# Expert inputs gathered as quarter rows per block of 32 tokens, turned by VectorE and scaled by GpSimd

## The reference, cut to what matters

```python
x = layer_norm(alpha * x + g2 * hier_moe(modulate(x, sh2, sc2), *moe_w), ln2_g[i], ln2_b[i])
# modulate(u, shift, scale) = normalize(u) * (1 + scale) + shift
# routed_experts: for each token t and each of its two experts e, weighted by gate:
#   h = silu(t @ w_gate[e]) * (t @ w_up[e]);   y = h @ w_down[e]
```

## Time and profile before

| | us |
|---|---|
| median of three runs | 1712.03 (1709.75 to 1712.45) |
| span of the profiled execution | 1710.9 |
| expert stage, first transposes to last down product | 1186 to 1648 |
| TensorE busy in the span | 1513.6 |
| VectorE, ScalarE, GpSimd busy | 928.0, 691.7, 209.5 |

### The profile page before, as it was taken

One profiled execution on the slowest core, in us unless ns is written; L12 is line 12 of the kernel. 1 busy time (PEld: TensorE's weight loads), 2 busy tenths in 40 slices (PEclk: granted clock), 3 DMA queues, 4 the chain that ended last, 5 costly groups with the idle time before them and its releaser, 6 DMA issues. The chain is left out here.

```text
span 1710.9 us, 47254 instructions
## 1 busy us (share of the span) xinstructions
PE 1513.6 (88%) x19436; PEld 1110.0 (65%) x19436; DVE 928.0 (54%) x1855; ACT 691.7 (40%) x1585; POOL 209.5 (12%) x274
## 2 busy tenths in 40 slices
PE   4799998999968899977999979873999999999868
PEld 2588886779857788864666667762555555555433
DVE  5798752331125556649999846666151543545416
ACT  5544431012334455435777724432142423443321
POOL 0000101000034535404000000000000000000014
PEclk9899999999977999999999989885999999999989
DMA  9312315551133344231011033316849589999976
GB/s 363 115 62 90 114 62 205 175 165 39 59 114 109 115 127 127 84 104 50 26 54 34 13 121 148 136 76 265 354 136 409 222 324 413 400 401 418 409 251 251
DMA packets 115267, 305.34 MB, mean 178 GB/s; under 512 B 11010, under 2 KB 57682, under 8 KB 106074
## 3 DMA queue, kind: packets, MB, share of 16 engines
q1 hardware_dynamic: 93178, 244.95, 37.8%
q0 software_dynamic: 10336, 46.67, 7.8%
q10 hardware_dynamic: 11520, 10.49, 2.0%
HBM read 256.41 MB, written 45.67 MB: 177 GB/s over the span
## 5 line engine op out<-in xcount | busy, mean ns | idle before, releaser
L2747 PE MATMUL psum<-now_hidden,i_xm 128*32 128x256 f32 x4992 | 291.0, 385 | 9.8 <-DVE now_hidden L2849 6.4
L2747 PEld LDWEIGHTS psum<-now_hidden,i_xm 128*32 128x32 f32 x4992 | 160.0, 111 | 132.0 <-issue 27.6
L2759 PE MATMUL psum<-now_down,i_hT 128*32 128x256 f32 x2464 | 147.7, 379 | 5.8 <-ACT now_down L2810 5.8
L2865 DVE TENSOR_TENSOR i_h<-i_silu,psum 128x128 f32<-128x128 f32 x78 | 22.2, 285 | 219.6 <-ACT i_silu L2803 219.6
L2793 ACT ACTIVATE i_xm<-psum,run_mod 128x128 f32<-128x128 f32 x163 | 63.3, 457 | 152.1 <-issue 125.7
L2759 PEld LDWEIGHTS psum<-now_down,i_hT 128*32 128x32 f32 x2464 | 81.4, 110 | 58.9 <-ACT now_down L2810 9.2
L2849 DVE COPY now_hidden<-raw_hidden 128x1024 f32 x168 | 104.4, 693 | 21.2 <-DMA raw_hidden<-in_w_up 11.9
L124 PE MATMUL psum<-hT_head,wm_head 128*128 128x512 f32 (+1 forms) x256 | 96.6, 377 | 11.8 <-DVE hT_rest L415 7.5
L1918 PE MATMUL psum<-dkT,f_qT 64*128 64x512 f32 (+1 forms) x384 | 90.7, 580 | 18.4 <-ACT f_E L1968 15.9
L1968 ACT ACTIVATE f_E<-psum,f_mx 128x1280 f32<-128x1280 f32 (+2 forms) x96 | 92.8, 971 | 19.9 <-DVE f_mx L2029 19.1
L124 PE MATMUL psum<-hT_head,wm_rest 128*128 128x512 f32 (+1 forms) x256 | 94.6, 369 | 0.0
(11 more groups left out here) (378 smaller groups left out, 3049.7 us busy)
## 6 DMA issues: line engine op xcount, KB each, us to landing
raw_hidden<-in_w_gate SPq DMA_DIRECT2D x22, 2048.0 KB, 25.0
raw_hidden<-in_w_up SPq DMA_DIRECT2D x22, 2048.0 KB, 29.5
raw_down<-in_w_down SPq DMA_DIRECT2D x22, 2048.0 KB, 19.9
wa_late<-in_w_ada POOLq DMA_DIRECT2D x16, 1024.0 KB, 6.9
yb<-i_y ACTq DMA_DIRECT2D x80, 128.0 KB, 11.5
wa<-in_w_ada SPq DMA_DIRECT2D x8, 1024.0 KB, 13.7
wt<-in_w_in SPq DMA_DIRECT2D x4, 2048.0 KB, 8.8
wm<-in_w_in SPq DMA_DIRECT2D x12, 512.0 KB, 3.8
```

Source lines behind the costliest of these rows:

```text
L2747: last = nc.tensor.matmul(by_blocks(hidden_bank(s)[j * SUB:(j + 1) * SUB, :]), xm[u][:, k, s * SUB:(s + 1) * SUB], columns_of(now["hidden" ...
L2759: last = nc.tensor.matmul(down_bank(s)[j * SUB:(j + 1) * SUB, :], hT[s % 2][:, k * SUB:(k + 1) * SUB], now["down"][:, k, j * WIDE:(j + 1) ...
```

## The change

Rows are gathered as quarters: `xn2` is seen as 4096 rows of 256 numbers, and a block of 32 tokens takes 128 of them, one per partition, the quarter a of token t on partition 32 a + t. `tok` so holds 4 token + quarter for each of 96 blocks and some beyond. The one-hot tiles are made per block (96) and row within a block (32), in plain float32, and each of the 16 picks is summed by four matmuls in column groups of 32. There are four tiles `xg` and four `xm`, one block each. VectorE turns a block by one instruction in 32x32 blocks, three blocks ahead, behind `keep_y`; GpSimd multiplies by the scale and adds the shift (two instructions, with a wait on its own semaphore between) and then issues the gather of a block four further on. TensorE's transposes and ScalarE's evictions are gone, and each block's hidden product waits for `x_kept`. At the start VectorE turns the first block ahead of its first copies of weights and the second behind them.

```diff
+QUARTER = 70
+AHEAD = 3
+RING = SUBS
+def quarters(ap):
+    return ap.rearrange("t (a n) -> (t a) n", a=SUBS)
...
-    xg = m.keep["xg"] = [m.sb(f"i_x{u}", [P, D]) for u in range(2)]
+    xg = m.keep["xg"] = [m.sb(f"i_x{u}", [P, D // SUBS]) for u in range(RING)]
-    part_hot, row_hot = m.sb("r_part_hot", [P, PICKS, QUADS], F32R), m.sb("r_row_hot", [P, PICKS, P], F32R)
+    part_hot, row_hot = m.sb("r_part_hot", [P, PICKS, BLOCKS]), m.sb("r_row_hot", [P, PICKS, SUB])
...
-        cp(tok[:, 0:QUADS], m.bank(2, QUADS)).then_inc(token_ready, 1)
+        ts(tok[:, 0:BLOCKS], m.bank(2, BLOCKS), float(SUBS), small[:, QUARTER:QUARTER + 1], ALU.mult, ALU.add).then_inc(token_ready, 1)
...
-            last = nc.tensor.matmul(m.bank(2, QUADS), row_hot[:, n, :], part_hot[:, n, :], start=(n == 0), stop=(n == PICKS - 1))
+            for a in range(SUBS):
+                last = nc.tensor.matmul(m.bank(2, BLOCKS)[a * SUB:(a + 1) * SUB, :], row_hot[:, n, :], part_hot[:, n, :], start=(n == 0), stop=(n == PICKS - 1),
+                                        tile_position=(0, a * SUB))
...
     @block.gpsimd
+        def gather(b):
+            pool.wait_ge(x_turned, b - RING + 1)
+            pool.indirect_dma_start(out=xg[b % RING][:, :], out_offset=None, in_=quarters(d["xn2"]),
+                                    in_offset=bass.IndirectOffsetOnAxis(ap=tok[:, b:b + 1], axis=0)).then_inc(gathered[b % RING], 16)
+        def each_row(w):
+            return run_mod[:, w, :].unsqueeze(2).to_broadcast([P, KD, SUB])
+        def modulate(b):
+            pool.wait_ge(x_turned, b + 1)
+            nc.gpsimd.tensor_tensor(xt[b % 2][:, :, :], xt[b % 2][:, :, :], each_row(1), ALU.mult).then_inc(x_scaled, 1)
+            if b >= RING:
+                pool.wait_ge(used["hidden"], (b - RING + 1) * KD)
+            pool.wait_ge(x_scaled, b + 1)
+            nc.gpsimd.tensor_tensor(xm[b % RING][:, :, :], xt[b % 2][:, :, :], each_row(0), ALU.add).then_inc(x_kept, 1)
+        def body(q, i, u, s):
+            b = q * SUBS + s + AHEAD
+            modulate(b)
+            gather(b + RING)
...
     @block.tensor
-        def turn_x(i, u):
-            pe.wait_ge(gathered[u], 16 * i + 16)
-            pe.wait_ge(x_kept[1 - u], i + u)
-            for k in range(KD):
-                last = nc.tensor.transpose(m.bank(k // 4)[:, k % 4 * P:(k % 4 + 1) * P], run_columns(xg[u], k), ident)
-            last.then_inc(x_turned[u], 1)
...
-            if r == 0:
-                pe.wait_ge(x_kept[v], i + u + 1)
+            pe.wait_ge(x_kept, b + 2)
...
     @block.scalar
-                last = nc.scalar.activation(xm[u][:, k, :], m.bank(k // 4)[:, k % 4 * P:(k % 4 + 1) * P], ACT.Identity,
-                                            scale=run_mod[:, 1, k:k + 1], bias=run_mod[:, 0, k:k + 1])
...
     @block.vector
+        def turn_x(b):
+            dve.wait_ge(gathered[b % RING], 16 * (b // RING) + 16)
+            if b >= 2:
+                dve.wait_ge(x_kept, b - 1)
+            nc.vector.transpose(xt[b % 2][:, :, :], run_columns(xg[b % RING])).then_inc(x_turned, 1)
...
             mix(b + 1, (s + 1) % SUBS)
             keep_y(b, i, u, s)
+            turn_x(b + AHEAD)
```

More of the change, by code:

```diff
@@ L2723, in _, with hidden @@
     def _(pool):
-        def gather(q, i, u):
-            pool.wait_ge(x_turned[u], i)
-            pool.indirect_dma_start(out=xg[u][:, :], out_offset=None, in_=d["xn2"],
-                                    in_offset=bass.IndirectOffsetOnAxis(ap=tok[:, q:q + 1], axis=0)).then_inc(gathered[u], 16)
+        def gather(b):
[15 more added lines that the diff above has]
+            gather(b + RING)
         pool.wait_ge(routed, 1)
+        pool.wait_ge(mod_ready, 1)
+        for b in range(AHEAD):
+            modulate(b)
+            gather(b + RING)
         nc.gpsimd.memset(nothing[:, :], 0.0).then_inc(nothing_ready, 1)
-        blocks(pool, start=lambda q, i, u: gather(q + 2, i + 1, u))
+        nb = blocks(pool, block=body)
+        for u in range(RING):
+            pool.wait_ge(gathered[u], ((nb + AHEAD + 2 * RING - 1 - u) >> 2) * 16)
     @block.tensor
     def _(pe):
-        def turn_x(i, u):
-            pe.wait_ge(gathered[u], 16 * i + 16)
-            pe.wait_ge(x_kept[1 - u], i + u)
-            for k in range(KD):
-                last = nc.tensor.transpose(m.bank(k // 4)[:, k % 4 * P:(k % 4 + 1) * P], run_columns(xg[u], k), ident)
-            last.then_inc(x_turned[u], 1)
-        def hidden(b, u, s, place, ks):
+        def hidden(b, s, place, ks):
             pe.wait_ge(copied["hidden"], place * KD + ks[-1] + 1)
@@ L2766, in body @@
             here, after = place_of(pe, b), place_of(pe, b + 1)
-            v, r = (u, s + 1) if s + 1 < SUBS else (1 - u, 0)
-            if r == 0:
-                pe.wait_ge(x_kept[v], i + u + 1)
+            r = (s + 1) % SUBS
+            pe.wait_ge(x_kept, b + 2)
             pe.wait_ge(mixed, b)
-            hidden(b + 1, v, r, after, range(KD // 2))
-            hidden(b + 1, v, r, after, range(KD // 2, KD))
+            hidden(b + 1, r, after, range(KD // 2))
+            hidden(b + 1, r, after, range(KD // 2, KD))
             down(b, s, here)
         pe.wait_ge(routed, 1)
-        turn_x(0, 0)
         first = place_of(pe, 0)
+        pe.wait_ge(x_kept, 1)
         for k in range(KD):
-            if k < KD - 1:
-                pe.wait_ge(first_kept, k + 1)
-            else:
-                pe.wait_ge(x_kept[0], 1)
-            hidden(0, 0, 0, first, range(k, k + 1))
-        blocks(pe, lambda q, i, u: turn_x(i + u, 1 - u), body)
+            hidden(0, 0, first, range(k, k + 1))
+        blocks(pe, block=body)
     @block.scalar
     def _(act):
-        def shape(i, u, ks):
-            if ks[0] == 0:
-                act.wait_ge(x_turned[u], i + 1)
-            for k in range(*ks):
-                last = nc.scalar.activation(xm[u][:, k, :], m.bank(k // 4)[:, k % 4 * P:(k % 4 + 1) * P], ACT.Identity,
-                                            scale=run_mod[:, 1, k:k + 1], bias=run_mod[:, 0, k:k + 1])
-                if i == 0 and u == 0 and k < KD - 1:
-                    last.then_inc(first_kept, 1)
-            if ks[1] == KD:
-                last.then_inc(x_kept[u], 1)
         def gate(b, s):
@@ L2893, in _ @@
         ahead = [after, look(2)]
+        turn_x(1)
         mix(0, 0)
+        for b in range(2, AHEAD):
+            turn_x(b)
         blocks(dve, block=body)
@@ L3054, in constants @@
     small[:, 69] = NORM_EPS
+    small[:, QUARTER] = i // SUB
     ids = (np.arange(P)[:, None] + P * np.arange(TL)[None, :]).astype(np.float32)
```

46 lines of the change are left out of this document (21 added, 25 removed).

## The result

The changed kernel is slower: 1717.5 us median of 20 runs against 1708.7, a ratio of 1.0046 (95% interval 1.0033 to 1.0059), about +8 us. One execution of the kernel before took 2505.8 us; the ratio compares fast executions alone. The profiled execution of the changed kernel took 1720.7 us, its span is 1718.9.

The account below looks back on a forecast made before the run. TensorE was taken to bound the expert stage up to 1411 us, shared with DMA to 1532, then DMA. Terms of +6.5, +4.0 and 0 gave +10.5 on a 1710.9 span, so 1722.5 us; range 1704 to 1732.

Parts of the forecast that it names:

- no change: Rival for the whole kernel: x about 0.6 to 0.8, terms cancel, 1711 to 1714 us; chance 0.09.
- Port cost x: Expert switches: GpSimd's two operations and gather lengthen each set of eight VectorE copies by 1.4 us (bounds 0 and 1.7).
- The turn: VectorE, each block: one more instruction of 256 elements, 0.5 us (bounds 0.4 and 0.8); 0.75 if strided reading is half speed.
- A wait: TensorE, each of a quad's four bodies: waiting for x_kept costs 0 to 0.15 us, taken as 0.06.
- a boundary: TensorE between quads: transposes and a wait leave, new waits come; 1.0 us saved each (bounds 0.65 and 1.24).
- The start: Expert stage's start: smaller one-hot products, then turns and copies on VectorE, delay the second hidden product by 2.3 us (-1 to +8).
- +4.0 up to 1532, nothing after: From 1411 to 1532 three pairs +9.0, five boundaries -5.0; after 1532 DMA is the bound, so neither counts.
- The pieces of 1 KB: Gathers on DMA: same bytes in 1 KB pieces, no loss, put at 0; 2 to 3 us if costing a half more.
- The tail: End of the expert stage: the tail's copy (+1) and its missing transposes (-1.1) cancel.
- the faster one: Rival: GpSimd costs copies little, x near 0, 1705.6 us; turning point x = 0.6 per set; chance 0.26.
- marks that I had named: Expert stage: copy sets 6.2 to 6.6 us, products 5.3 to 5.4 apart, now_hidden idle 40 or more, start 2 to 3 later.
- Starving: Rival: GpSimd's second tensor_tensor gets no turn between eight copies, TensorE idles on i_xm; 1728 us, chance 0.07.

Follow-up runs that it names:

- few gathers: Changed kernel, GpSimd gathering only for blocks that will be turned (up to nb + 2, not nb + 6), without the final wait; 1.0009 of the kernel before.
- the stop at nb: Changed kernel, blocks past nb neither gathered, turned nor scaled, 78 gathers, without the final wait; 1.0006 of the kernel before.
- a lead of six: GpSimd's operations held back to run beside the gated product, six blocks ahead, TensorE's x-tile wait dropped for blocks 9 to 60; 0.9934 of the kernel before, 1699.1 us.
- a lead of four: Changed kernel stopping at nb, four blocks ahead, GpSimd's operations held back to run beside the gated product, TensorE's waits kept; 0.9976 of the kernel before.

## Why the prediction was right, and by which steps

The time (1722.5 forecast, about 1717.5 measured) and the sign hold. So does the mechanism as far as it goes: GpSimd's arithmetic slows VectorE's copies, and TensorE waits for the copied weights in chains of switches. Without that arithmetic the ratio is 0.9988 in place of 1.0046 (some 3 to 4 us of it by the better covered drain).

But that this outweighs the transposes isn't shown, and the sign owes much to luck. The kernels with few gathers and with the stop at nb keep all of the arithmetic, only the drain is moved, and they take 1.0009 and 1.0006 of the time before, with 1 inside both intervals. From the stage's first load to h77 it is 472.4 us before, 477.3 after, and 474.9 and 473.5 in these two: up to there the slower copies and the saved transposes nearly cancel, which is the case "no change" that I had given 0.09. The 6 of 8 us that are clear of noise are the drain, a cost that the forecast put at nothing. By steps:

- *Port cost x, 1.4 us per set.* Measured 0.95: 0.87 for the arithmetic, under 0.1 for the gather, where I had 0.28. The two do take turns, as the earlier trace rows suggested, but a turn costs the copies 0.43 us each and not the whole length of GpSimd's operation; the 0.27 us in the earlier trace rows is not there either once a gather starts later in the set. Between two sets of a chain lie 1.34 us, not 1.63. With the terms below it makes -0.3 us from h2 to h41, where +4.2 was forecast.
- *The turn, 0.5 us.* Measured 0.64, within the bounds; the term for VectorE's own part was too small by 0.14. A step does cost here: 0.21 us of the 0.64. The Trainium skill's rule on steps over 16 bytes ("SBUF — State Buffer", Door 1) has the right sign, and my estimate from it, 0.75, came a little nearer than 0.5. The strided reduce of the earlier trace rows was no evidence of a free step.
- *A wait, 0.06 us.* Measured 0.13, so a boundary saves 1.24 - 0.52 = 0.7, at my lower bound.
- *The start, +2.3.* Measured from the stage's first load: +0.3 for the first hidden product, -0.4 for the second and to h2. The 128 small weight loads took 5.00 us (6.4 forecast), 1.5 us more than before; but the first gather of 1 KB rows had landed and its turn began 6.5 us after its issue, not 8.3 as with the 4 KB rows. The second block's turn did stand behind the first copies, as foretold, and cost TensorE the one wait of 0.8 us; the eight transposes that stood there before had cost 1.1.
- *+4.0 up to 1532, nothing after.* h41 to h77 is 5.5 us longer, so the sum nearly holds, but not by the chains it was worked out from: without GpSimd's arithmetic, with sets of 5.0 us, this stretch is still 3.9 us longer than before. What I had named as its mark did not show either: DMA share from 1411 to 1532 stayed at 1.00. What makes the stretch longer stays open. A full DMA does not by itself make TensorE's time free: with a lead of six the last 36 blocks took 5.8 us less than with a lead of four.
- *The pieces of 1 KB, 0.* Holds: queue 0 needs 7.6% of the engines' span for 11200 packets, where it needed 7.8% for 10336. But not by my working with a quarter of a packet's time: the trace has no packets of 1 KB on this queue. The last gather of the changed kernel is 32 packets of 4096 bytes and 16 of 4 bytes, the last of the kernel before 128 and 16, most of the large ones 0.2 us in both.
- *The tail, "cancel".* Wrong: +8.0 us from h77 to met. 6.5 of them are the omitted term, GpSimd's drain, 82.4 ns for each of 84 gathers, put behind the last gather's landing; the rest lies between h77 and TensorE's own drain. I had said that four issues on POOL instead of one "stand behind nothing that is due", and had not read how the stage ends.

Errors of x, the wait, the start and the tail have both signs and largely cancel; the number was better than its terms, by luck. Of the rivals, the faster one is refuted in its place (x of 0.95 is above its turning point of 0.6) but points to what was true in another order: products that read PSUM and transposes slip past GpSimd freely. Of the marks that I had named, TensorE's grown wait for the copied weights (52 us) and the end of the 6.4 us steps came; the sets stayed short of 6.2, the products were 5.42 to 5.45 apart, and the first one was only 0.3 us late. Starving did not occur: one wait of 0.8 us.

## What to carry to other kernels

Before moving arithmetic to GpSimd, look at which VectorE instructions run beside it: behind a dependence its start is often pinned to the worst one, and one more wait that moves it beside transposes or PSUM reads can turn a loss into a gain. Small gathers cost VectorE's copies little here while they run (under 0.1 us per set) and were paid when GpSimd drained at the end of the program block: let its last work end early enough to hide that, and look there before predicting. A wait that is always met still costs TensorE; a longer lead that lets another wait imply it is worth having where TensorE sets the pace.

## What the runs showed of the hardware that was not expected

- GpSimd's drain at the end of the expert block lasts about 82.4 ns per gather issued in it, if the last of them has landed: 6923 ns for 84 (with arithmetic or without), 6594 for 80, 6431 for 78 (in two kernels; 6507 in a third), 8148 for 99, 1937 for 23. There it doesn't matter how long ago they were (the last was issued 4 to 31 us before the drain) or how large. Where the drain begins with the last gather still under way it is longer: 9816 ns for 80, 9067 and 8354 for 81, and in the kernel before 10.4 us for 22, which ended 0.95 us behind that gather's landing. How landing and count add up was not worked out. The drain of the last phase, 3769 ns with 16 gathers of another kind that had long landed, does not follow the rule and is unexplained.
- An fp32 copy within SBUF on VectorE (128x1024, 614 ns from one to the next) is slowed by GpSimd's tensor_tensor: eight of them take 5.86 us instead of 4.99. A transpose within SBUF (0.31 and 0.64 us) and a tensor_tensor with an input in PSUM (0.39) are not.
- ScalarE's activation of 128x32 out of SBUF took 401 ns; the evictions of 128x128 out of PSUM in the kernel before took 457. By these two rows a small tile costs ScalarE nearly as much as one four times as wide.
